# One-hots of 4 tokens per instruction with the gates scaled by ScalarE, 3 key blocks per slab and 12 behind, cache copies beside top-k, 80 candidate sums, 24 rows fetched early

## The reference

```python
q = (tok @ w_q).reshape(n, PEER_HEADS, 2, PEER_DKEY // 2)
s1 = einsum('nhk,ek->nhe', q[:, :, 0], sk[0]); s2 = einsum('nhk,ek->nhe', q[:, :, 1], sk[1])
v1, i1 = top_k(s1, 16); v2, i2 = top_k(s2, 16)
cand = v1[..., :, None] + v2[..., None, :]            # 16 x 16 sums
top_s, top_i = top_k(cand.reshape(n, 8, 256), 16)
expert = i1 * 128 + i2 at top_i;  gate = softmax(top_s)
act = gelu(einsum('nd,nhkd->nhk', t, u_tab[expert]))
out = einsum('nhk,nhkd->nd', gate * act, v_tab[expert])
```

## Time and profile before

| | us |
|---|---|
| median of 3 runs | 2494.01 (2491.13 to 2499.25) |
| profiled execution | 2512.14, of it span 2510.3 |

### The profile page before, as it was taken

How to read it: one execution, slowest core, us unless ns; L and a number is a source line. 1 busy time by engine, 2 the same in 40 slices (tenths; PEclk the granted TensorE clock), 3 DMA queues, 4 the chain that set the end, 5 groups by cost and what they waited for, 6 DMA issues and landing times.

```text
span 2510.3 us, 36519 instructions
## 1 busy us (share of the span) xinstructions
PE 2153.8 (86%) x12253; PEld 1789.4 (71%) x12253; DVE 1598.4 (64%) x3547; ACT 745.1 (30%) x1111; POOL 801.0 (32%) x499
## 2 busy tenths in 40 slices
PE   7999999986789863999999888888579889889893
PEld 7999955553433343999999888888557677667672
DVE  1284145545432320179888687777778889889897
ACT  2232124433310011234444344444222323223221
POOL 2333300001100011346666511111434336566550
PEclk9999989988889986999999988888789999999896
DMA  7676658849979796235555576666799999999992
GB/s 270 242 245 239 236 222 336 320 160 329 320 288 332 277 344 207 75 108 171 171 171 172 187 257 234 235 227 226 293 366 395 395 395 390 391 392 378 394 394 91
DMA packets 200412, 682.70 MB, mean 272 GB/s; under 512 B 18432, under 2 KB 84352, under 8 KB 194304
## 3 DMA queue, kind: packets, MB, share of 16 engines
q1 hardware_dynamic: 151696, 508.36, 57.1%
q0 software_dynamic: 46080, 167.79, 17.7%
q10 hardware_dynamic: 2544, 5.48, 0.6%
HBM read 618.78 MB, written 196.32 MB: 325 GB/s over the span
## 4 chain that ended last, share of the span: by engine, by line
PE 44%; DMA 20%; issue 19%; DVE 12%; ACT 3%; POOL 1%; SPq 1%; DVEq 0%; ACTq 0%; POOLq 0%
DMA overlay<-peer_v 13%; PE bank L188 10%; PE bank L189 10%; PE bank L190 10%; DMA overlay<-peer_u 4%; DVE arena L1760 3%; PE bank L1746 3%; DVE overlay L1915 2%; DVE arena L1755 2%; PE bank L601 2%; PE bank L585 2%; POOL overlay L1404 1%; PE bank L624 1%; ACT arena L1698 1%; PE bank L651 1%
## 5 line engine op out<-in xcount | busy, mean ns | idle before, releaser
L188 PE MATMUL bank<-overlay 128*128 128x384 f32 (+4 forms) x2856 | 987.2, 346 | 141.1 <-DVE overlay L1918 115.1
L189 PE MATMUL bank<-overlay 128*128 128x384 f32 (+4 forms) x2856 | 971.3, 340 | 0.0
L190 PE MATMUL bank<-overlay 128*128 128x384 f32 (+4 forms) x2856 | 968.4, 339 | 0.0
L188 PEld LDWEIGHTS bank<-overlay 128*128 128x128 f32 x2856 | 558.4, 196 | 194.3 <-issue 130.6
L190 PEld LDWEIGHTS bank<-overlay 128*128 128x128 f32 x2856 | 556.9, 195 | 33.8
L189 PEld LDWEIGHTS bank<-overlay 128*128 128x128 f32 x2856 | 558.5, 196 | 31.3
L1404 POOL TENSOR_TENSOR overlay<-overlay 128x1024 fp32r<-128x1024 f32 x99 | 266.5, 2694 | 260.6 <-ACT overlay L1396 260.6
L1608 POOL DMA_INDIRECT arena<-peer_rows,arena x160 | 165.2, 1032 | 459.2 <-DVE arena L1755 441.5
L1608 POOL DMA_INDIRECT arena<-peer_v,arena x160 | 237.1, 1482 | 161.6 <-DVE arena L1760 146.5
L1755 DVE SCALAR_TENSOR_TENSOR arena<-arena 128x1024 f32<-128x1024 f32 x160 | 195.6, 1227 | 18.6 <-DMA arena<-peer_rows,arena 18.5
L1760 DVE SCALAR_TENSOR_TENSOR arena<-arena 128x1024 f32<-128x1024 f32 x160 | 206.0, 1288 | 0.0
(11 more groups left out here) (221 smaller groups left out, 2107.3 us busy)
## 6 DMA issues: line engine op xcount, KB each, us to landing
overlay<-peer_u SPq DMA_DIRECT2D x128, 512.0 KB, 3.7
overlay<-peer_v SPq DMA_DIRECT2D x128, 512.0 KB, 10.5
o_ks<-cache_k SPq DMA_DIRECT2D x16, 4088.0 KB, 18.5
o_vsall<-cache_vall SPq DMA_DIRECT2D x16, 4088.0 KB, 59.7
arena<-cache_kT SPq DMA_DIRECT2D x32, 896.0 KB, 11.0
arena<-cache_v SPq DMA_DIRECT2D x56, 512.0 KB, 6.6
arena<-w_out SPq DMA_DIRECT2D x48, 512.0 KB, 6.3
act<-arena SPq DMA_DIRECT2D x128, 192.0 KB
```

What stands on the lines that cost most here:

```text
L188: pe.matmul(out, lhs[0], rhs[0], start=start, stop=False)
L189: pe.matmul(out, lhs[0], rhs[1], start=False, stop=False)
L190: return pe.matmul(out, lhs[1], rhs[0], start=False, stop=stop)
```

## The change

Six edits go together.

1. The 5 cache copies of the w_out stage and the 6 of the query stage are issued by ScalarE on its own queue, beside top-k: four in each of the first two groups of 16 key blocks, one in each of the three dense ones.
2. Of the 256 candidate sums per head only 80 are formed and searched: row 0 in full, rows 1 to 7 to column 7, column 0 of the rest. The index arithmetic takes six more small instructions.
3. 24 of the gathered rows are fetched early into a ring of 4 (`ering`), by GpSimd between its low halves, and VectorE takes their dots between the searches of the dense tiles, behind every 14th search.
4. One-hots are made for the 4 tokens of a window in one instruction each, without the gate; ScalarE multiplies the gate in, token by token (`scale`).
5. A slab has 3 key blocks (UPS) instead of 4, in the order `ORDER_IN_SLAB`, and 12 blocks stand behind the slabs (TAIL = 116). The first loads for the values and the first gates are issued among them.
6. The rows on VectorE are dealt anew: 24 early, 60 in the slabs, 24 in the tail, 212 in the value stage (LATE_ROWS) instead of 256. Most loops of these stages are written out.

```diff
-                if c % 3 == 2:
-                    copy_cache(sp, 1, 7 + c // 3)
...
-            for x in (5, 6, 12, 13, 14, 15):
-                copy_cache(sp, 1, x)
...
-            with pool.Fori(0, (QF + EARLY) // 4) as x:
+            with pool.Fori(0, (QF + 2 * AHEAD) // 4) as x:
                 for s in range(4):
                     lo(x * 4 + s, s)
+            pool.wait_ge(topk.sem, after["sparse"])
+            for n in range(DT * AHEAD):
+                lo(QF + 2 * AHEAD + n, n % 4)
+                if n % 2 == 0:
+                    g = n // 2
+                    if g >= 4:
+                        pool.wait_ge(erow_done, g - 3)
+                    pool.indirect_dma_start(ering[g % 4], None, t["peer_rows"], bass.IndirectOffsetOnAxis(ap=rows3[:, g:g + 1], axis=0))\
+                        .then_inc(erow_in[g % 4], 16)
...
+        FULL = TOPK // 2
+        CAND = TOPK + (FULL - 1) * FULL + TOPK - FULL
+        cand = cut(111, PH, CAND)
...
+        PER_ROWS, APART = TOPK // 2, 14
+        EARLY_ROWS = DT * PER_ROWS
...
+            def between(row):
+                searched[0] += 1
+                if row and searched[0] % APART == 0 and searched[0] // APART <= PER_ROWS:
+                    row(searched[0] // APART - 1)
...
+                step(dve.tensor_tensor(cand[:, :, 0:TOPK], v[:, :, 0, 0:1].to_broadcast([P, PH, TOPK]), v[:, :, 1], ALU.add))
...
+                def early_dot(r):
+                    at = ering[r % 4].rearrange("p (b n) -> p b n", b=2)
+                    dve.wait_ge(erow_in[r % 4], i * (16 * PER_ROWS // 4) + 16 * (r // 4 + 1))
+                    dve.scalar_tensor_tensor(at, at, 1.0, bank[:, 4:6, :], ALU.mult, ALU.mult, accum_out=w3[:, bass.ds(i * PER_ROWS + r, 1)]).then_inc(erow_done, 1)
...
-        assert EARLY + SLABS * GRP == PK
+        UPS = 3
+        TAIL = EARLY + SLABS * UPS
+        ORDER_IN_SLAB = ("u0", 0, 1, 2, "u1", 3, 4, 5, "u2", 6, 7)
...
+            def keep_slab(n):
                 sp.wait_ge(g_kept, n * GS + (GS + 2))
-                sp.dma_start(t["gate"][bass.ds(n, 1)].rearrange("s p a n -> p (s a) n"), slab[s]).then_inc(slab_stored[s], 16)
-
-            def last_rows(n, first=False, more=True):
-                for s in range(4):
-                    if more:
-                        a = n * 4 + (EARLY + s + 4)
-                        fetch(a, s, (u_lo, QF + EARLY + s + 1) if first and s < LEAD else (u_lo2, n * 4 + (s + 1 - LEAD)))
-                    keep(n * 4 + (EARLY + s), s, n + EARLY // 4)
-
-            last_rows(0, True)
-            with sp.Fori(0, (SLABS - 2) // 2) as x:
-                for s in range(2):
-                    keep_slab(x * 2 + s, s)
-                    last_rows(x * 2 + (s + 1))
-            keep_slab(SLABS - 2, 0)
-            last_rows(SLABS - 1, more=False)
+                sp.dma_start(t["gate"][n], slab[n % 2]).then_inc(slab_stored[n % 2], 16)
+
+            def next_row(a):
+                if a + 4 < PK:
+                    fetch(a + 4, a % 4, (u_lo, QF + a + 1) if a < EARLY + LEAD else (u_lo2, a - (EARLY + LEAD) + 1))
+                keep(a, a % 4, a // 4)
+
+            for n in range(SLABS):
+                if n:
+                    keep_slab(n - 1)
+                for k in range(UPS):
+                    next_row(EARLY + n * UPS + k)
...
-            keep_slab(SLABS - 1, 1)
+            keep_slab(SLABS - 1)
+            for a in range(TAIL, PK):
+                next_row(a)
+                if a == TAIL + 3:
+                    sp.wait_ge(slab_stored[1], 16 * (1 + SLABS // 2))
+                    sp_gates(sp, 0, 0)
...
+                    if n % 4 == 0 and n // 4 < len(copies):
+                        copy_cache(act, 1, copies[n // 4])
-                block(i, i * SPARSE_TILE + after["shifted_sparse"])
+                block(i, i * SPARSE_TILE + after["shifted_sparse"], [i * 4 + (5 + k) for k in range(4)])
             with act.Fori(0, DT) as i:
-                block(i + 2, i * PER_TILE + after["shifted"])
+                block(i + 2, i * PER_TILE + after["shifted"], [i + 13])
...
+            def scale(w):
+                act.wait_ge(hot_made, w + 1)
+                for j in range(4):
+                    mm = act.activation(hot_b[:, w % 2, j], hot_b[:, w % 2, j], ACT.Copy, scale=slotT[:, 2, w * 4 + j:w * 4 + j + 1])
+                mm.then_inc(hot_ready, 1)
...
+            scale(0)
+            for n in range(SLABS):
+                for what in ORDER_IN_SLAB:
+                    if isinstance(what, str):
+                        next_row(EARLY + n * UPS + int(what[1]))
+                        continue
+                    w = n * GS + what
+                    if w + 1 < SLABS * GS:
+                        scale(w + 1)
+                    if what == 0:
+                        act.wait_ge(slab_stored[n % 2], 16 * (n // 2 + 1))
+                    act.wait_ge(g_done, w + 3)
+                    act.copy(slab[n % 2][:, :, 4 * what:4 * what + 4].rearrange("p a n -> p n a"),
+                             bank[:, 4 + w % 2, :].rearrange("p (n a) -> p n a", a=P)).then_inc(g_kept, 1)
...
-                    for j in range(4):
-                        at = lambda row: slotT[:, row, bass.ds(w * 4 + j, 1)]
-                        dve.tensor_scalar(hot_a[:, par, j], const("iota"), at(0), None, ALU.is_equal)
-                        mm = dve.tensor_scalar(hot_b[:, par, j], const("iota"), at(1), at(2), ALU.is_equal, ALU.mult)
-                    mm.then_inc(hot_ready, 1)
...
+                    token = lambda row: slotT[:, row, w * 4:w * 4 + 4].unsqueeze(2).to_broadcast([P, 4, P])
                     dve.wait_ge(g_done, w + 1)
+                    dve.tensor_tensor(hot_b[:, w % 2], over(const("iota")), token(1), ALU.is_equal)
+                    dve.tensor_tensor(hot_a[:, w % 2], over(const("iota")), token(0), ALU.is_equal).then_inc(hot_made, 1)
+                    if k in (0, 3, 6):
+                        low(EARLY + n * UPS + k // 3 + LEAD)
+                    if k in (1, 2, 4, 5, 7):
+                        g = n * 5 + (1, 2, 4, 5, 7).index(k)
+                        rows_of(g, g + 1)
...
+        LATE_ROWS = 2 * UROWS - EARLY_ROWS - DONE
...
+                rows_here = range(a * LATE_ROWS // PK, (a + 1) * LATE_ROWS // PK)
```

More of the change, by code:

```diff
@@ L1498, in fence, with top16 @@
                 dve.memset(small(900 + len(fences), 1), 0.0)
-            def top16(values, width, out_v, out_i, n):
+            def top16(values, width, out_v, out_i, n, row=None):
                 for k in range(2):
@@ L1504, in top16 @@
                         step(dve.max(out_v(f, k), values(f)))
+                        between(row)
                     fence()
@@ L1735, in pe_up, with next_row @@
             pe.wait_ge(ch_kept, DT + 1)
-            def slab_rows(n, first=False):
-                for s in range(4):
-                    low = (u_lo, QF + EARLY + s + 1) if first and s < LEAD else (u_lo2, n * 4 + (s + 1 - LEAD))
-                    up(n * 4 + (EARLY + s), s, low)
-                    for par in range(2):
-                        w = n * GS + (2 * s + par)
-                        pe.wait_ge(hot_ready, w + 1)
-                        pe.wait_ge(g_kept, w + 1)
-                        for j in range(4):
-                            mm = pe.matmul(bank[:, 4 + par, j * P:(j + 1) * P], hot_b[:, par, j], hot_a[:, par, j], start=True, stop=True)
-                        mm.then_inc(g_done, 1)
-            slab_rows(0, True)
-            with pe.Fori(1, SLABS) as n:
-                slab_rows(n)
+            def next_row(a):
+                up(a, a % 4, (u_lo, QF + a + 1) if a < EARLY + LEAD else (u_lo2, a - (EARLY + LEAD) + 1))
+            for n in range(SLABS):
+                for what in ORDER_IN_SLAB:
+                    if isinstance(what, str):
+                        next_row(EARLY + n * UPS + int(what[1]))
+                        continue
+                    w = n * GS + what
+                    pe.wait_ge(hot_ready, w + 1)
+                    pe.wait_ge(g_kept, w + 1)
+                    for j in range(4):
+                        mm = pe.matmul(bank[:, 4 + w % 2, j * P:(j + 1) * P], hot_b[:, w % 2, j], hot_a[:, w % 2, j], start=True, stop=True)
+                    mm.then_inc(g_done, 1)
+            for a in range(TAIL, PK):
+                next_row(a)
         def dot(dve, r, turn, h, w, j):
@@ L1785, in dve_onehots, with low @@
-            with dve.Fori(0, SLABS // 2 - 1) as x:
-                for n2 in range(2):
-                    for s in range(4):
-                        quarter(x, n2, s, False)
-            for n2 in range(2):
-                for s in range(4):
-                    quarter(SLABS // 2 - 1, n2, s, True)
-            for g in range(SLAB_ROWS, SLAB_ROWS + 2 * RING):
-                dot(dve, g % RING, g // RING, h1[:, DT], w3, g)
+            def low(a):
+                if EARLY + LEAD <= a < PK:
+                    dve.wait_ge(u_hi, QF + a + 1)
```

(28 more changed lines are left out.)

159 lines of the change are left out of this document (75 added, 84 removed).

## The result

The changed kernel takes 2609.18 us (median of four runs, 2602.26 to 2612.88) where the kernel before takes 2494.0 on the same chip: ratio 1.0456, 95% interval 1.0428 to 1.0485. It is 115 us slower. The forecast was slower by 47, with its own range at 2490 to 2595, so the time lies above that, and 1 us inside the whole range of 2440 to 2610. The profiled execution took 2612.88 us (span 2611.0), 100.7 more in span than that of before.

The account below looks back on a forecast made before the run. Bounds were taken per stage, such as TensorE in key blocks and DMA in values. Terms -18 - 53 + 27 + 49 + 100 - 59 = +46 gave 2494 + 47 = 2541 us; range 2440 to 2610.

Parts of the forecast that it names:

- The bound of each stage: Whole kernel: which engine or wait holds each stage, such as TensorE in the key blocks and DMA in the values.
- w_out and queries (-71): w_out and query stages: stalls go when the copies leave, 18 us saved in the first and 53 in the second.
- Copies beside top-k (+27, bounds 0 and +50): Key blocks beside top-k: copies on ScalarE's queue make peer_u loads land late, costing 27 us.
- the rule: Key blocks: two blocks need one landing plus 1.9 us of ScalarE; 8.4 us of TensorE cover landings up to 6.5.
- the 10 us of absorption: Key blocks beside top-k: the three blocks TensorE has ready absorb some 10 of the 37 us lost to copies.
- Rival 3: Copies beside top-k share DMA fairly, so a load lands in 4.4 us and 27 us go: 2514; chance 0.10.
- Early rows (+49): Dense tiles: early gathered rows arrive late and TensorE waits for top-k, 16 us in each of three tiles.
- Rival 2: Dense tiles: the early rows are not late, so the term of 49 goes: 2492; chance 0.08.
- Slabs and tail (+100): Slabs and tail: scalings and the load behind the store lengthen slabs to 37.6 us; 506 us against 406.
- rival 1: Slabs: the stage does not lengthen, the load lands in time, slabs of 28.6 us: 2440; chance 0.20.
- Values (-59): Value stage: bound by DMA, 44 gathered rows of 0.52 MB fewer save 59 us.
- Rival 4: Slabs: TensorE's clock stays at its lower level, 1.2 of 2.4 GHz, adding up to 150 us: 2640; chance 0.12.

Follow-up runs that it names:

- run 1: The changed kernel with all 11 cache copies back on SP in the w_out and query stages: 2596.7 us, ratio 1.0407 to the kernel before.
- run 4: The kernel before with only the 11 copies moved to ScalarE's queue beside top-k: 2516.0 us, ratio 1.0067.
- run 3: The changed kernel with each copy beside top-k issued as four quarter DMAs, one per key block, pieces still 32 KB: 2584.7 us.
- run 5: The changed kernel with GpSimd's early gathers issued three rows ahead among the low halves: 2577.8 us.
- run 6: The changed kernel with SP issuing the slab's store behind the next peer_u load instead of ahead of it: 2523.3 us.
- runs 6 to 8: First run 6; second, the changed kernel with gates multiplied by VectorE instead of ScalarE's scalings, 2549.1 us; third run 8.
- run 2: The changed kernel with the 11 copies beside top-k cut into 4 KB pieces instead of 32 KB: 3073.4 us, ratio 1.2293.
- run 10: The kernel of run 8 with its quarter copies thinned out, 16 of 44 moved beside the query blocks: 2380.0 us, ratio 0.9525.
- run 8: The changed kernel with quarter copies, gathers three rows ahead, store behind the load and gates on VectorE: 2411.4 us, ratio 0.9673.

## Why the prediction was right on the sign and 68 us short

**The bound of each stage, and w_out and queries (-71): right.** -73.1 measured, inside the bounds. The 61.4 us wait for peer_wq is gone. With run 1 the copies account for 63 of it; the other 10 are the difference between that kernel and the one before in the same code. Together with the 9.6 of the first stage they come to 19 us, about as much as the profiled execution of before lay above its median. So they are probably that execution's lateness and not the change's gain, which no run shows.

**Copies beside top-k (+27, bounds 0 and +50): here it failed.** Measured +79 in the changed kernel (run 1) and +87 alone (run 4), outside the bounds. The mechanism and the rule were right: two blocks need one landing plus 1.9 us of ScalarE. The landing put into the rule was wrong. I took 11.6 us, the median of the o_hs stores of the earlier trace rows, and then a pace from the bytes, 21.4 us per four blocks (its two terms, 13.1 and 8.7, make 21.8, and the term +30). The load waits for the whole copy, as the upper end of that same row said (17.8): it lands at 1069.17, 1.2 us behind the copy. The copy's packets are 8 times as large as peer_u's and 8 of them are queued on every engine (128 over 16); with two on each the median landing is 8.3 us (run 3). That the engines take turns by packet fits this and is not shown by it. With 17.1 the pair of blocks behind a copy needs 19.0, the pair without one some 6 (its loads have landed meanwhile), and four blocks 25: seen 25.3. Eight times 8.5 are 68; the 32 blocks of the sparse tiles took 66 more than in run 1 (198.5 against 132.3), so nearly none of the 10 us of absorption was there. The other 13 fell in the dense tiles, whose copies I had called absorbed. Rival 3, a fair share, is refuted: it had the load land in 4.4 us, and not 27 us went but 52 came on top.

**Early rows (+49): right.** +47 by run 1, TensorE waiting 15.4 and 16.1 us at the end of a tile for the 16 forecast, VectorE for peer_rows ahead of it. Run 5, which changes only the order of the gathers, gives back 31. Rival 2 is refuted with it.

**Slabs and tail (+100): mechanism right, 14 too small.** The period is 37.4 us for the 37.6 worked out, 28.9 for 28.6 without the stall (run 6), so rival 1, decided at 33, is refuted. The scalings at 1.27 us a window were priced at 1.24. What is missing lies outside the eleven periods: slot copy to first store is 39.8 us (35.5 before), where the sum had a slab of 28.6, and last store to the first value block 69.8 (40.0 before), where it had 64. In the tail ScalarE waited up to 12.6 us for peer_u behind the last stores, while DMA moved 341 GB/s, not the 390 that the term divided by. The two parts of the slab term, the store's stall and the scalings, are told apart by runs 6 to 8: a slab takes 28.9 us without the first, 31.1 without the second, 24.2 without both.

**Values (-59): right**, -56.5.

**The base.** The profiled execution of before was 9.6 us late when w_out began. The span difference of 100.7 is 110.3 without that offset, 64 more than the sum of +46: 52 of them are the copies, 14 the slabs and the tail, and the other terms take 2 off. From there to the 115 of the medians 5 are left, within the spread of the runs. The sum itself is +46; the 47 that the prediction added to 2494 is 1 us off it.

**Rival 4, the clock.** The granted clock of the slabs is 0.84, after 0.89. TensorE is at half speed for the windows behind the 8.63 us stall (16 matmuls in 3.74 us at 1669.45, as in the earlier trace rows) and back at full speed in the next key block, whose matmuls from 1673.21 take 0.34 us each. Over the slabs 83 us of TensorE's busy time fell into stretches at half speed (60 before), which makes some 41 us longer work, 3.5 a slab. So the clock cost a few us a slab and not whole blocks.

## What to carry to other kernels

Before a large transfer is moved beside latency-bound loads, count not only its bytes but how many pieces of what size it queues on each engine: a load that is issued behind it waits for them all, and the buffers ahead must cover that whole time. Spreading the pieces in time helps, most where the bytes fit under the compute of every step; making them smaller can cost far more. And when an engine takes a second job in a chain in order (here the gate scalings behind a high half), look for the load at the head of that chain: a swap of two DMA issues on SP was worth 86 us, more than the 47 forecast for the whole change.

## What the runs showed of the hardware

- An HBM to HBM copy in packets of 4088 bytes took 3.3 times as much of the engines' time for its bytes, with loads beside it, as one in packets of 32704: 0.63 us of an engine per packet against 1.50 (run 2). The loads' own packets of 4096 bytes suffered as well, 0.48 us each instead of 0.20. Whether the small packet costs that much by its size or by where it starts, and by itself or only between packets of another queue, no run here tells.
- With a whole copy of 32 KB packets on another queue, the load of 512 KB behind it landed after 17.1 us, and the median load of that stretch after 14.6; with a quarter of the copy per key block the median was 8.3 (run 3); with a quarter on every second key block 4.8 (run 10); and with no copy beside it 3.6.
- A tensor_tensor of 128x512 with a broadcast operand takes 0.68 us as is_equal and the same 0.68 as mult (run 8, L1842 to L1845); the dearer price of a product in the earlier trace rows does not hold for this shape.
